# High weights first in each half of a weight product: reordering TensorE's products and splitting their wait

## The reference

```python
def first_block(...):
    proj = rms_norm(h, attn_norm) @ w_in
    ...
    h = h + jnp.concatenate([y_mla, y_swa], axis=-1) @ w_out[l]
    m = rms_norm(h, mlp_norm[l])
    h = h + jnp.square(jax.nn.relu(m @ w_up[l])) @ w_down[l]
def second_block(...):
    h = h + hybrid_mixer(...)              # w_in_2, w_out_2
    h = h + memory_cross_attention(...)    # xa_wq, xa_wk, xa_wv, xa_wo
    h = h + squared_relu_mlp(...)          # mlp_w1, mlp_w2
```

## Time and profile before

| | us |
|---|---|
| time of three executions | 2587.63, 2585.65, 2586.31 (median 2586.31) |
| span of the profiled execution, first to last instruction | 2585.4 |
| TensorE busy in it (a modelled figure: products are pipelined) | 2558.9 |
| VectorE busy | 1659.7 |
| ScalarE busy | 1347.0 |
| DMA | 182 GB/s on average, 470.77 MB |

### The profile page before, as it was taken

How to read it: one execution, slowest core, us unless ns; L and a number is a source line. 1 busy time by engine, 2 the same in 40 slices (tenths; PEclk the granted TensorE clock), 3 DMA queues, 4 the chain that set the end, 5 groups by cost and what they waited for, 6 DMA issues and landing times.

```text
span 2585.4 us, 33847 instructions
## 1 busy us (share of the span) xinstructions
PE 2558.9 (99%) x13780; PEld 2157.7 (83%) x13780; DVE 1659.7 (64%) x2128; ACT 1347.0 (52%) x1907; POOL 0.2 (0%) x4
## 2 busy tenths in 40 slices
PE   9999999999999999999999999999999999999998
PEld 7878888888888888887888888888888888888887
DVE  7686566655655566668788967544556655665565
ACT  6665554444444446568866665544454444444444
POOL 0000000000000000000000000000000000000000
PEclk9999999999999999999999999999999999999999
DMA  6534676566556655555454437544555565556554
GB/s 225 171 123 146 214 225 200 192 196 193 188 190 194 195 187 174 195 179 179 134 187 147 147 131 252 179 147 145 191 192 191 194 195 188 189 194 196 189 187 145
DMA packets 235041, 470.77 MB, mean 182 GB/s; under 512 B 8235, under 2 KB 17158, under 8 KB 233478
## 3 DMA queue, kind: packets, MB, share of 16 engines
q1 hardware_dynamic: 234134, 467.04, 55.2%
q10 hardware_dynamic: 752, 1.58, 0.2%
HBM read 462.30 MB, written 6.29 MB: 181 GB/s over the span
## 4 chain that ended last, share of the span: by engine, by line
PE 49%; DVE 1%; ACT 0%; issue 0%; DVEq 0%
PE ps L1267 10%; PE ps L1269 10%; PE ps L1268 10%; PE ps L1306 9%; PE ps L1305 5%; PE ps L1659 1%; PE ps L1839 1%; PE ps L1814 1%; PE ps L1338 0%; PE ps L1713 0%; PE ps L1597 0%; PE ps L1588 0%; PE ps L1750 0%; PE ps L1640 0%; PE ps L1736 0%
## 5 line engine op out<-in xcount | busy, mean ns | idle before, releaser
L2652 DVE TENSOR_TENSOR WL<-Wt,WH 128x1024 fp32r<-128x1024 f32 (+1 forms) x861 | 1037.2, 1209 | 708.7 <-ACT WH L1894 657.2
L1894 ACT ACTIVATE WH<-Wt 128x1024 fp32r<-128x1024 f32 (+1 forms) x861 | 894.5, 1046 | 769.9 <-PE ps L1269 508.4
L1267 PE MATMUL ps<-WH,XT 128*128 128x512 f32 (+1 forms) x1184 | 470.8, 398 | 1.6 <-DVE WL L2652 1.3
L1267 PE MATMUL ps<-WH,HT 128*128 128x512 f32 (+2 forms) x1176 | 457.1, 389 | 3.2 <-DVE WL L2652 3.2
L1269 PE MATMUL ps<-WH,XT 128*128 128x512 f32 (+1 forms) x1184 | 459.4, 388 | 0.0
L1268 PE MATMUL ps<-WL,XT 128*128 128x512 f32 (+1 forms) x1184 | 458.9, 388 | 0.0
L1269 PE MATMUL ps<-WH,HT 128*128 128x512 f32 (+2 forms) x1176 | 451.5, 384 | 0.0
L1268 PE MATMUL ps<-WL,HT 128*128 128x512 f32 (+2 forms) x1176 | 451.0, 384 | 0.0
L1306 PE MATMUL ps<-XT,WH 128*128 128x512 f32 x960 | 336.5, 394 | 0.0
L1306 PE MATMUL ps<-HT,WH 128*128 128x512 f32 x960 | 336.5, 394 | 0.0
L1305 PE MATMUL ps<-HT,WL 128*128 128x256 f32 x960 | 266.6, 278 | 0.0
(11 more groups left out here) (404 smaller groups left out, 1887.4 us busy)
## 6 DMA issues: line engine op xcount, KB each, us to landing
Wt<-in_mlp_w SPq DMA_DIRECT2D x128, 1024.0 KB, 5.2
Wt<-in_w_up SPq DMA_DIRECT2D x64, 1024.0 KB, 5.4
Wt<-in_w_down SPq DMA_DIRECT2D x64, 1024.0 KB, 5.1
Wt<-in_w_in SPq DMA_DIRECT2D x53, 1024.0 KB, 5.2
Wt<-in_w_out SPq DMA_DIRECT2D x32, 1024.0 KB, 5.1
Wt<-in_xa_wk SPq DMA_DIRECT2D x16, 1024.0 KB, 5.1
Wt<-in_xa_wv SPq DMA_DIRECT2D x16, 1024.0 KB, 5.1
Wt<-in_xa_wq SPq DMA_DIRECT2D x16, 1024.0 KB, 5.1
```

What stands on the lines that cost most here:

```text
L1267: pe.matmul(o, xh, wh, start=start, stop=False)
L1894: act.activation(m.WH[:, i % NR, 0:2 * w], m.Wt[:, slot % NW, h * 2 * w:(h + 1) * 2 * w], ACT.Copy).then_inc(*up("wsplit.a", i))
L2652: dve.tensor_tensor(m.WL[:, i % NR, 0:2 * w], m.Wt[:, slot % NW, h * 2 * w:(h + 1) * 2 * w], m.WH[:, i % NR, 0:2 * w].bitcast(F32), SUB).t ...
```

## The change

`half` and `half_turned` go through their products twice. The first pass has all products with the high weights and waits for ScalarE's `wsplit.a` (and, as before, for the rows and for the freed banks). The second has those with the low weights and waits for VectorE's `wsplit.v`. The products are the same in number and size; `half_block`, the form for the last halves of the last down product, is left as it is.

```diff
     def half(x):
-        for kk in range(2):
...
-                pe.matmul(o, xh, wh, start=start, stop=False)
-                pe.matmul(o, xh, wl, start=False, stop=False)
-                done = pe.matmul(o, xl, wh, start=False, stop=stop)
-                if kk == 1 and tb == 1:
-                    done.then_inc(*up("gemm.t", x.i))
+        for lows in range(2):
+            for kk in range(2):
...
+                for tb in range(2):
...
+                    if lows:
+                        on.wait_ge(*(at("wsplit.v", 0, kk) if x.i == 0 else at("wsplit.v", x.i)))
+                        done = pe.matmul(o, xh, wl, start=False, stop=stop)
+                        continue
+                    on.wait_ge(*(at("wsplit.a", 0, kk) if x.i == 0 else at("wsplit.a", x.i)))
+                    on.wait_ge(*at(*rows_sig(x.key, kt)))
+                    if start:
+                        for s in freed(x.acc[tb]):
+                            on.wait_ge(*s)
+                    pe.matmul(o, xh, wh, start=start, stop=False)
+                    pe.matmul(o, xl, wh, start=False, stop=False)
+        done.then_inc(*up("gemm.t", x.i))
```

```diff
     def half_turned(x):
-        for n in range(4):
-            o = m.bank(x.acc[n])
-            for kk in range(2):
...
-                pe.matmul(*(both if start else one), start=start, stop=False)
-                done = pe.matmul(*(one if start else both), start=False, stop=stop)
-            done.then_inc(*up("gemm.t", "own", x.i, n))
+        for lows in range(2):
+            for n in range(4):
+                o = m.bank(x.acc[n])
+                for kk in range(2):
...
+                    if lows:
+                        on.wait_ge(*at("wsplit.v", x.i))
+                        done = pe.matmul(o[:, 0:256], wl, XX[:, 0, kt, :], start=False, stop=stop)
+                        continue
+                    on.wait_ge(*at("wsplit.a", x.i))
+                    on.wait_ge(*at(*rows_sig(x.key, kt)))
+                    if start:
+                        for s in freed(x.acc[n]):
+                            on.wait_ge(*s)
+                    pe.matmul(o.rearrange("p (a t) -> p a t", a=2), wh, XX[:, :, kt, :], start=start, stop=False)
+                if lows:
+                    done.then_inc(*up("gemm.t", "own", x.i, n))
```

More of the change, by code:

```diff
@@ L1254, in half @@
     def half(x):
-        for kk in range(2):
[L1256 to L1266, removed]
-                pe.matmul(o, xh, wh, start=start, stop=False)
-                pe.matmul(o, xh, wl, start=False, stop=False)
-                done = pe.matmul(o, xl, wh, start=False, stop=stop)
-                if kk == 1 and tb == 1:
-                    done.then_inc(*up("gemm.t", x.i))
+        for lows in range(2):
+            for kk in range(2):
+                kt = x.k2 + kk
+                wh, wl = (t[:, x.i % NR, kk * x.w:(kk + 1) * x.w] for t in (m.WH, m.WL))
+                start, stop = x.first and kk == 0, x.end and kk == 1
+                for tb in range(2):
+                    o = m.bank(x.acc[tb])[:, 0:x.w]
+                    xh, xl = (m.moving(x.key, part, kt)[:, tb * P:(tb + 1) * P] for part in range(2))
+                    if lows:
[10 more added lines that the diff above has]
+        done.then_inc(*up("gemm.t", x.i))
         M.note("gemm.t", "end", x.key)
@@ L1290, in half_turned @@
         XX = m.HT if x.key[:2] == "m1" else m.XT
-        for n in range(4):
-            o = m.bank(x.acc[n])
-            for kk in range(2):
[L1294 to L1304, removed]
-                pe.matmul(*(both if start else one), start=start, stop=False)
-                done = pe.matmul(*(one if start else both), start=False, stop=stop)
-            done.then_inc(*up("gemm.t", "own", x.i, n))
-            if n == 3:
+        for lows in range(2):
+            for n in range(4):
+                o = m.bank(x.acc[n])
+                for kk in range(2):
+                    kt = x.k2 + kk
+                    c = kk * x.w + n * P
+                    wh, wl = (t[:, x.i % NR, c:c + P] for t in (m.WH, m.WL))
+                    start, stop = x.first and kk == 0, x.end and kk == 1
+                    if lows:
[10 more added lines that the diff above has]
+                    done.then_inc(*up("gemm.t", "own", x.i, n))
+            if lows:
                 M.note("gemm.t", x.i)
```

## The result

The changed kernel takes 2602.48 us (median of 4 runs, 2601.23 to 2605.14), beside 2586.01 us of the kernel before on the same chip (2585.65 to 2587.63). The ratio is 1.0063, interval 1.0051 to 1.0075: slower by 16.5 us, where the prediction had 9.0 us and a range up to 2600 us. The direction was right, the size was not.

What follows compares the result with a forecast made beforehand. TensorE, busy 99% of the span, was taken as the bound, with 4.6 us of low-weight waits as the prize. Terms +1.3 + 8.0 + 0.5 + 0.5 - 1.3 = +9.0 us gave 2595.3 us against 2586.31, range 2587 to 2600 us.

Steps and rivals of the forecast that it cites:

- Term 2: Behind up chunks, at d0 to d6 and u1 of both MLPs: waits for bank evacuation, 16 x 0.50 us, +8.0 us.
- Term 1: Pace of products in the 256 turned halves, long and short ones now in separate runs: +1.3 us, at most 2.6.
- Terms 3 and 4: Banks wanted sooner in u0's first chunk, 0.25 us twice, +0.5 us; rows wanted sooner at 254.03 us, +0.5 us.
- Term 5: Gains from starting high products early: 1.3 us at the kernel's start, should last; mixer taken as 0, given back.
- The hidden evacuation: Rival at the up chunks' ends: evacuation stays hidden, 2587.3 us, or half hidden, about 2591 us; chance 0.23 together.
- the gain kept in the mixer: Rival: the mixer's gained waits for low weights stay gained, 3.7 us, giving 2581.3 us; chance 0.04.
- late weights: Rival: bunched evacuation delays the weights, a second wait of about 0.5 us at 16 places, 2603 us; chance 0.08.
- loads at 0.19 us: Rival: stationary operand loads set the pace of short products in turned halves, 154 us more, 2740 us; chance 0.01.

## Why the prediction was right and wrong

**What bounds the kernel, right.** The prize was the 4.6 us of waits for low weights, and none of it was kept.

**Term 2, the wait right, its size 1.4 us short.** 0.50 us at 16 places was predicted: 0.39 us at the start of the product that waits and 0.11 us at the one behind it. The start of a down product, against that of before, moves by 0.49 us at each of d0 to d6 in both MLPs and by 0.43 us at u1, 7.7 us in all. The half behind that start loses another 0.10 to 0.12 us (0.09 in u1), 1.7 us in all. Together that is 9.4 us against 8.0, and it is by chance that 0.49 looks like the predicted 0.50. Three steps of the chain came out as predicted, at all 16 places: 0.32 us to ScalarE's start, 0.41 to VectorE's, 0.42 for the addition. The fourth did not: I had 0.05 us from the release to TensorE's start, from a wait for low weights, and here it is 0.15 us (404.21 to 404.37). Why it differs stays open. Going back to the order of before in the last half gave 6.9 us back (8.3 by the ratios); delaying block 0 by three short products added 0.36 us per place; dealing the banks otherwise moved the waits to other products. So the chain is shown, with its fourth step mis-sized.

**Term 1, the step that failed most.** I took +1.3 us, at most 2.6, "the sum is 0.34 to 0.35 us for a pair", from rows where at most two short products stand together. In the change four halves take 11.17 us (388.98 to 400.15, starts of the rows of eight short products), 2.793 us each. Before, two halves take 5.54 us (364.82 to 370.36), 2.77 each. With 2.774 from full timelines (364.82 to 392.56 is 27.74 us for ten) the difference is 0.019 us for a steady half. Not every half loses that much. All 256 together lose 11.7 us from start to start, of which 7.7 are the waits, 0.2 the product behind the wait in u1 and 0.6 the first halves of u0; so 3.3 us are left for the pace, 2.0 us more than the term and 0.7 us more than the most I had allowed it. The mechanism that I dismissed, the load's pace, has a part in it. I had ruled out 0.19 us and stopped there; what had to be asked is whether load and stream, so close to each other (0.11 and 0.11 us), still overlap in a long row. The pairs that I read it from do not show that: the load of the first short product can be done beside the long one ahead of it.

**Terms 3 and 4, right.** u0 loses 0.28 us in its first half where I had 0.25 us. In w_out the wait for `XT` now leaves eight products behind it: its recorded wait went from 0.28 us to

```profile
253.58 0.50 PE L1272 MATMUL ps<-WH,XT 128*128 128x512 f32 x1 [0.75 <-DVE XT L3056]
```

and the next halves are 0.44 us later, against 0.5.

**Term 5, wrong at both places.** Of the start I wrote "it should last". Half 1 did start early:

```profile
10.65 0.39 PE L1273 MATMUL ps<-WH,XT 128*128 128x512 f32 x1
11.80 0.39 PE L1272 MATMUL ps<-WH,XT 128*128 128x512 f32 x1
...
14.52 0.39 PE L1272 MATMUL ps<-WH,XT 128*128 128x512 f32 x1
```

0.73 us ahead of 12.53 and 0.89 us at the next half (14.52 against 15.41). It was not the 1.3 us of the term, as in this execution the products of half 0 followed each other every 0.42 us until 10.65, before only until 8.64; half 1 has no wait ahead of it. In three other kernels with the early start it began 1.0 to 1.2 us early. The gain was used up at 28 us:

```profile
28.12 0.26 PE L1354 MATMUL ps<-CST,GR 112*128 112x112 f32 x1
29.49 0.30 PE L1356 MATMUL ps<-CST,GR 96*128 96x96 f32 x1 [1.10 <-DMA GR<-in_cf_dw_w]
...
29.76 0.47 PE L1272 MATMUL ps<-WH,XT 128*128 128x512 f32 x1
```

Before, that half started at 29.33, so 0.4 us are lost where I had 1.3 us gained. The loss itself isn't the early start's: the two kernels without it (the order in `half_turned` alone, the order without the early start) lose 0.5 us at these transposes too. The transfer was issued on SyncE at the same time in both (21.90 and 21.95 us): I had looked for TensorE's later waits for engines, and not for the transfer that was just in time.

In the mixer I took 0, as the gain is given back at the transposes. It is, and the rows show how:

```profile
1287.90 0.43 PE L1272 MATMUL ps<-WH,HT 128*128 128x352 f32 x1
...
1290.22 0.91 PE L1265 MATMUL ps<-WL,HT 128*128 128x352 f32 x4 [0.78 <-DVE WL L2658]
1293.29 0.88 PE L1565 MATMUL ps<-CST,QA 128*128 128x128 f32 x6 [2.17 <-DVE QA L3210]
```
```profile
1292.02 1.22 DVE L3210 TENSOR_TENSOR QA<-QA,QE 128x1024 f32<-128x1024 f32 x1
```

VectorE's L3210 is 5.67 us later than its counterpart before (1286.35), by what TensorE had lost until then. TensorE in front of it got through faster and then stood for 2.17 us where it had stood for 0.90. I priced the pause by what it delays. But the clock fell at it: in 1294 to 1297.5 us products of 352 columns follow each other every 0.29 us in place of 0.16. Apart from that the mixer is even: what its waits gain up to 1287 us, the longer pause takes back.

**The sum and the base.** 7.7 + 1.7 + 3.3 + 0.6 + 0.4 = 13.7 us; with the start at +0.4 it is 14.1 us, and the profiles are 14.0 us apart. Each has one stretch at the lower clock, of about 1.6 us, so that these two cancel. That of before lies elsewhere, at 155.6 us behind a pause of 1.6 us, and was not among my rows:

```profile
150.00:162.00 12.00, 10.40 (x57) 7.94 (x56) 8.95 (x23) 4.14 (x9) 0.00 (x0) 0.86 0.37 129
```

The span was forecast at +9.0 us and is 5.0 us above that: 2.0 us are term 1's, 1.7 us the start's and 1.4 us term 2's. None of the three alone would have left the range; together with the next point they did. (The terms at their upper ends add up to 2599.0 us, not to the 2599.5 of the forecast's own range.)

The median is off by another 2.2 us. The runs of before come in two groups by their clock, 2585.5 to 2586.6 us at a mean granted clock of 0.999, and 2587.1 to 2588.1 us at 0.998 (few lie outside). By its span the profiled execution of before belongs to the second group, and its time was about 2587.2 us, while the median of 2586.01 us is of the first. So "what lies around the span" is 1.8 us and not 0.9, and the 0.9 us came from setting a median of one group beside a span of the other. The change's median lies 1.2 us above its profiled execution as well. 14.0 + 1.2 + 1.2 us are the 16.5 us of the medians but for rounding.

By experiment, 13.8 of the 16.5 us are the order's, and 2.6 us come with the early start. The profile has 1.6 us of these in the mixer, at the lower clock. The last 1.0 us is not settled, and medians of four and five runs can differ by as much.

**The rivals.** The hidden evacuation, the gain kept in the mixer, late weights (nothing waits twice) and loads at 0.19 us did not come about. Nor does a satisfied wait cost anything: halves of the form `half` take 2.72 us before and after.

## What to carry to other kernels

Grouping products by what they wait for also groups their ends: work that was emptied block by block behind TensorE now comes all at once at the end, and the first to need a bank pays the whole chain of ScalarE and VectorE (0.5 to 0.6 us at 16 places here, with what the next products lose). Short products should stay between long ones here: in a row of eight they run at 0.12 us each, and a half takes 2.79 us in place of 2.77. A wait taken from a bound engine is only worth what the next wait doesn't take back (an engine's, a transfer's or a pause's), and several short waits made into one of 2.2 us can cost more than they did apart (1.6 us here, by the clock). And a time worked out from a profile's span wants the time of that same execution beside it, not the median.

## What the runs showed of the hardware

- Products with a load of a stationary operand of 128 columns each follow each other about every 0.11 us when they have 128 columns, though each load is recorded with 0.19 us; in a row with products of 256 columns the step is 0.12 us, with 512 columns 0.23 us. Why 0.12 and not 0.11 stays open.
- The granted clock fell to 0.51 (1.2 GHz) for some 3.5 us (6.7 in one) at a pause of 2.2 us of TensorE in the mixer, in seven of eight kernels that had it, and at the shorter pauses of 0.9 us at the same place in none of four. At two other pauses of 2.1 and 2.2 us (197 us with the transposes one half later, 30 us with the last half in the old order) it fell both times. At the pause of 1.6 us that eleven of the twelve kernels have at 155 to 158 us it fell in two, the kernel before and the new order in `half_turned` alone. In the run with the transposes one half later it also fell at 34.4 us with no pause over 0.7 us close ahead of it. So a pause of one length can go either way, and a long one isn't needed. One such stretch costs about 1.6 us, which is also the distance between the two groups of runs of the kernel before.
- A product that waits for VectorE starts 0.05 us after its release at the waits for low weights and rows, and 0.15 us after it at the 16 waits for the evacuation. The one behind it comes 0.07 to 0.11 us later than usual.
